# Order of matmuls in a narrow half, fewer fill matmuls between two stages, and a second load of x in pieces

## Chip, cores and metric

One core of one Trainium2 chip runs the whole program. The time is that of the device, in microseconds, from the first to the last instruction of one execution with what lies around it; the figure of a kernel is the median of its runs.

## What is computed

One layer of a streaming encoder on x (1, 256, 2048), everything in float32:

```python
h = rmsnorm(x, norm_mix_pre)
z, xbc, dt, q, k, v, q_idx, k_idx, w_idx, gates = split(h @ w_in)      # 18576 columns
y_ssm  = ssd_mixer(z, xbc, dt, ...) @ w_ssm_out                        # Mamba-2 branch, 4096 -> 2048
y_attn = dsa_mixer(q, k, v, q_idx, k_idx, w_idx) @ w_attn_out          # top-k attention, 2048 -> 2048
merged = sigmoid(gA) * y_ssm + sigmoid(gB) * y_attn
x = x + rmsnorm(merged @ w_mix_out, norm_mix_post)
h = rmsnorm(x, norm_ffn_pre)
x = x + rmsnorm((gelu(g) * val) @ w_down, norm_ffn_post)               # g, val = conv(h @ w_up)
```

Nearly all the work is products of 256 rows with about 340 MB of weights, each read once.

## The kernel before, in words

**Precision by two parts.** Each float32 weight w is split into a high part w_hi, rounded by ScalarE to the format that TensorE multiplies at one column per cycle (line 516), and a low part w_lo = w - w_hi, made by VectorE (line 892). Activations are split in the same way: a row tile of h_s, y_s or o_s holds 256 columns of high parts and 256 of low parts. A product is high times high, plus weight high times activation low, plus weight low times activation high.

**Halves.** The unit of the schedule is a *half*: 512 columns by 128 partitions of w_hi and of w_lo, 256 KB of weights. There are 1,224, and the table HALF (lines 74 to 81) numbers them by stage: Q 136, S 320, G 128, O 192, M 64, U 256, D 128. Four slots of w_hi and w_lo and four slots of raw weights (two halves each) go round. SP starts the loads of pair u when VectorE has finished half 2u - 7 (`slot_free`, line 309: lo_done at 2u - 6). ScalarE and VectorE work LEAD = 3 halves ahead of TensorE. ScalarE may overwrite a slot when TensorE has signalled `half_used` for the half four back.

**Narrow and wide.** In the stages Q, S and U the result is wanted with its channels on the partitions. There the weights are the stationary operand and the activations are streamed: `half`, lines 1448 to 1459, with two output tiles (banks b0 and b1) and two k-tiles. The high weights stream 512 columns (both parts of the activation), the low ones 256, into the bank's right half: eight matmuls, 4 x 512 + 4 x 256 = 3,072 columns. In the stages G, O, M and D the activations are stationary and 512 weight columns are streamed: `wide_half`, lines 1461 to 1472, six matmuls of 512 columns, three on one bank and then three on the other.

**Around the change.** Stage O ends with 16 halves on o_s; its halves on y_s are used 16 halves before stage M begins. The bytes of y_s are then used again: x_again (the second copy of x, for the residual sum), mix_gain and others lie on it. GpSimd loads them: it waits until TensorE has used all halves before M (line 475) and starts the two loads of x_again of 1 MB (line 477) and the 1 MB row of norm_mix_post, spread over the partitions (line 478). VectorE needs mix_gain behind half 16 of stage M (line 1308), and x_again at the end of stage M (line 1315), as does GpSimd (line 481). ffn_gain follows at the end of stage M (line 480).

Between M and U the new x (x2 = gained * scale + x_again) is made in pieces: VectorE takes seven (line 1320), GpSimd three (line 491). TensorE transposes it (h2_bank, line 1703, 16 tiles), ScalarE makes the high parts (line 795), VectorE the low parts (line 1329), and the first turn of U begins when the parts of tiles 0 and 1 are there, with the later tiles made between its halves. Ahead of the transposes TensorE runs six matmuls on `ones` and x_again into bank 7, whose result nobody reads (lines 1706 and 1707).

Of the kernel before, what the change touches and what calls it, by code (L numbers as in the profile page):

```python
# [73 lines left out]
HALF, TILE = {}, {}  # L74
# [46 lines left out]
def build(nc, x, norm_mix_pre, norm_mix_post, norm_ffn_pre, norm_ffn_post, w_in, b_gate, conv_xbc_w,  # L121
# [3 lines left out]
    with ctx:  # L125
        def sem(name):
            return ctx.enter_context(nc.semaphore(name))
# [7 lines left out]
        def place(name, shape, dt, at):  # L135
            size = 2 if dt == BF16 else 4
            for s in shape[1:]:
                size *= s
            at = (at + 31) // 32 * 32
            assert at + size <= ARENA, name  # L140
            return nc.alloc_sbuf_tensor_at(name, shape, dt, offset=base + at), at + size
# [37 lines left out]
        x_again, at = place("x_again", [P, 2, D], F32, RY)  # L179
# [61 lines left out]
        hi_done, lo_done, half_used = sem("hi_done"), sem("lo_done"), sem("half_used")  # L241
# [4 lines left out]
        par_in, small_in, skip_in, cs_kept, x_again_in = (sem(n) for n in (  # L246
            "par_in", "small_in", "skip_in", "cs_kept", "x_again_in"))
# [42 lines left out]
        x_view = x.rearrange("a (s p) d -> p (a s) d", p=P)  # L290
# [98 lines left out]
        def _(pool):  # L389
# [16 lines left out]
            for s in range(2):  # L406
                pool.tensor_scalar(x_rows[:, s, 3 * X_CHUNK:D], x_rows[:, s, 3 * X_CHUNK:D], stat[:, 0, 10 + s:11 + s], None,
                                   ALU.mult).then_inc(xn_pool, 1)
            rows = {"mix_pre": norm_mix_pre, "ffn_pre": norm_ffn_pre, "xbc_b": conv_xbc_b,
                    "ssm_norm": ssm_norm, "ffn_b": conv_ffn_b, "xbc_w": conv_xbc_w, "ffn_w": conv_ffn_w}  # L410
# [4 lines left out]
            for name, a in rows.items():  # L415
                src = rows_of(a)
                r0, n = PAR[name], src.shape[0]
# [54 lines left out]
                    pool.tensor_tensor(sq_sum[:], sq[:, 0, :] if n == 0 else sq_sum[:], sq[:, (n + 1) % 2, :],  # L472
                                       ALU.add).then_inc(sq_added, 1)

            pool.wait_ge(half_used, HALF["M"])
            for s in range(2):
                pool.dma_start(x_again[:, s, :], x_view[:, s, :]).then_inc(x_again_in, 16)
            pool.dma_start(mix_gain[:], norm_mix_post.rearrange("a d -> (a d)").partition_broadcast(P)).then_inc(gain_in[0], 16)
            pool.wait_ge(half_used, HALF["U"])
            pool.dma_start(ffn_gain[:], norm_ffn_post.rearrange("a d -> (a d)").partition_broadcast(P)).then_inc(gain_in[1], 16)  # L480
            pool.wait_ge(x_again_in, 32)
            pool.wait_ge(tile_out, TILE["M"] + 8)
            pool.wait_ge(inverted, 1)
            for n, (q, t) in enumerate(((1, 1), (3, 0), (3, 1))):
# [400 lines left out]
        def _(dve):  # L885
# [134 lines left out]
            with dve.Fori(0, 4) as i:  # L1020
                links.enter(i, 0, 8)
                for j in range(16):
# [10 lines left out]
                    if j % 8 == 7:  # L1033
                        for t in range(2):
                            k = j // 8
# [103 lines left out]
            with dve.Fori(0, GROUPS) as i:  # L1139
                links.enter(i, 0, 14)  # L1140
                for j in range(40):
# [41 lines left out]
                    if j % 8 == 7:  # L1183
                        k = j // 8
# [23 lines left out]
            with dve.Fori(0, GROUPS // 2) as i:  # L1208
                links.enter(i, 0, 2)
                for k in range(2):  # L1210
                    for j in range(16):
# [5 lines left out]
                        if 9 <= j < 13:  # L1217
                            n = 4 * k + j - 9
# [3 lines left out]
                        if 10 <= j < 14:  # L1222
                            n = 4 * k + j - 10
# [70 lines left out]
            def inverse(use):  # L1294

                dve.wait_ge(rooted, use + 1)
                dve.reciprocal(stat[:, use, 12:14], stat[:, use, 10:12]).then_inc(inverted, 1)
                dve.wait_ge(inverted, use + 1)
# [13 lines left out]
            with dve.Fori(1, 2) as i:  # L1312
                mix_turn(i, False)
            inverse(0)
            dve.wait_ge(x_again_in, 32)
            dve.wait_ge(tile_out, N + 8)

            def second_x(t, c0, c1):
# [120 lines left out]
            for n in range(8):  # L1439
                t, q = n // 4, n % 4  # L1440
# [6 lines left out]
        def _(pe):  # L1447
            def half(i, per, c, src, k0, b0, b1, start):

                pe.wait_ge(lo_done, i * per + (c + 1))  # L1450
                for k in range(2):
                    for t, b in enumerate((b0, b1)):
                        pe.matmul(bank[b][:], w_hi[:, c % 4, k, P * t:P * t + P], src[:, k0 + k, :],  # L1453
                                  start=start and k == 0, stop=False, skip_group_check=True)
                for k in range(2):
                    for t, b in enumerate((b0, b1)):
                        last = pe.matmul(bank[b][:, T:2 * T], w_lo[:, c % 4, k, P * t:P * t + P], src[:, k0 + k, 0:T],  # L1457
                                         start=False, stop=True, skip_group_check=True)
                last.then_inc(half_used, 1)
# [14 lines left out]
            def mm(o, a, b, start=True):  # L1474
                return pe.matmul(o, a, b, start=start, stop=True, skip_group_check=True)  # L1475
# [26 lines left out]
            for p in range(9):  # L1502
                if p >= 2:
                    pe.wait_ge(tile_out, 2 * p - 2)
                for j in range(8):
                    if p == 0:
                        pe.wait_ge(h_split, 2 * j + 2)
                    b = 2 * ((p + 1) % 2)
                    half(0, 0, 8 * p + j, h_s, 2 * j, b, b + 1, j == 0)
                    if p == 0 and j < 6:  # L1510
                        for kt in (2 * j + 4, 2 * j + 5):
# [38 lines left out]
            with pe.Fori(0, 4) as i:  # L1550
                for k in range(2):
                    pe.wait_ge(tile_out, i * 4 + (18 + 2 * k - 2))
                    for j in range(8):
                        half(i, 16, 72 + 8 * k + j, h_s, 2 * j, 2 * k, 2 * k + 1, j == 0)
# [148 lines left out]
                    last = pe.transpose(bank[4 + kt % 4][:, P * t:P * t + P], x2[:, t, P * kt:P * kt + P], ident[:])  # L1703
                last.then_inc(h2_mm, 1)

            for n in range(6):
                mm(bank[7][:], ones[:], x_again[:, 0, 0:WIDE])
            for kt in range(4):
                h2_bank(kt)
# [55 lines left out]
```

## Time and profile before

| | |
|---|---|
| median of 3 runs | 1825.42 us (1824.72 to 1825.81) |
| the profiled execution | 1825.45 us, of which the span of the trace is 1823.8 us |
| busy: TensorE | 1797.7 us, 99% |
| busy: VectorE | 1305.3 us, 72% |
| busy: ScalarE | 1098.7 us, 60% |
| busy: GpSimd | 159.3 us, 9% |
| HBM read | 342 MB, 189 GB/s over the span |

In the rows PE is TensorE, PEld its weight loads, DVE VectorE, ACT ScalarE, POOL GpSimd and SP SyncE. Matmuls are pipelined: the length of one is its time in flight, and the distance from start to start is what it costs. The timeline merges neighbours of one kind into one line with a count. The idle time in brackets counts from the end of the flight before. The clock is the one granted to TensorE, as a share of 2.4 GHz.

### The profile page before, as it was taken

Reading aid. Unit: us, or ns where it says so; the run is one execution under the profiler, and the core shown is the slowest. Engines: PE = TensorE matmul, PEld = TensorE weight load, DVE = VectorE, ACT = ScalarE, POOL = GpSimd, SP = SyncE. Lnnn points to the kernel's source line nnn. Section 1 sums busy time; section 2 is a strip of 40 time slices with the busy share of each in tenths; the row PEclk is TensorE's granted clock in tenths of the full one; section 3 lists DMA queues with packets and bytes.
Section 4 is the critical chain, followed back from the end, with each engine's and each line's share of the span. In section 5 each row is a group of like instructions: output and inputs, shape, how many; then the busy total and the mean of one; then the engine's idle time right before and its main releaser. Section 6 shows DMA issues by size and latency. Waiting matters only on the chain.

```text
span 1823.8 us, 34379 instructions
## 1 busy us (share of the span) xinstructions
PE 1797.7 (99%) x9519; PEld 1528.3 (84%) x9519; DVE 1305.3 (72%) x2436; ACT 1098.7 (60%) x2147; POOL 159.3 (9%) x230
## 2 busy tenths in 40 slices
PE   8999999999999999999999999999999999999997
PEld 7888888888888888888888888877888888888886
DVE  6766687888888788777755555555787888875555
ACT  6554566666666666666755455544766666665443
POOL 2000001110110010111100000001111111110000
PEclk9999999999999999999999999999999999999999
DMA  7656666766666665666666666676566666666664
GB/s 215 205 165 186 184 180 179 202 184 177 196 184 190 178 202 163 189 201 202 198 198 191 186 195 189 213 230 187 159 188 189 189 186 188 189 184 190 195 193 148
DMA packets 362387, 345.00 MB, mean 189 GB/s; under 512 B 29072, under 2 KB 291360, under 8 KB 361568
## 3 DMA queue, kind: packets, MB, share of 16 engines
q1 hardware_dynamic: 357024, 325.14, 60.1%
q0 software_dynamic: 5280, 19.23, 3.3%
q8 instruction: 25, 0.41, 0.1%
q14 instruction: 26, 0.21, 0.0%
q10 hardware_dynamic: 32, 0.01, 0.0%
HBM read 342.13 MB, written 2.16 MB: 189 GB/s over the span
## 4 chain that ended last, share of the span: by engine, by line
PE 90%; DVE 4%; issue 2%; ACT 2%; DMA 1%; DVEq 0%; ACTq 0%; SPq 0%
PE bank L1468 37%; PE bank L1453 32%; PE bank L1457 16%; PE bank L1475 3%; ACT w_hi L516 1%; DVE w_lo L892 1%; DVE cc L1080 1%; DMA raw<-in_w_mix_out 1%; PE bank L1592 0%; DVE xc L1091 0%; DMA x_rows<-in_x 0%; DVE upad L898 0%; DVE out_t L1442 0%; DVE bc L1091 0%; ACT cc L626 0%
## 5 line engine op out<-in xcount | busy, mean ns | idle before, releaser
L892 DVE TENSOR_TENSOR w_lo<-raw,w_hi 128x512 fp32r<-128x512 f32 x1224 | 855.0, 707 | 471.1 <-ACT w_hi L516 464.4
L516 ACT ACTIVATE w_hi<-raw 128x512 fp32r<-128x512 f32 x1224 | 760.7, 629 | 505.5 <-PE bank L1468 273.3
L1453 PE MATMUL bank<-h_s,w_hi 128*128 128x512 f32 x1824 | 508.2, 400 | 0.8 <-DVE h_s L910 0.8
L1453 PEld LDWEIGHTS bank<-h_s,w_hi 128*128 128x128 f32 x1824 | 312.3, 189 | 48.7 <-issue 5.2
L1468 PE MATMUL bank<-w_hi,y_s 128*128 128x512 f32 x1024 | 316.7, 389 | 0.0
L1457 PEld LDWEIGHTS bank<-h_s,w_lo 128*128 128x128 f32 x1824 | 278.9, 188 | 39.0
L1457 PE MATMUL bank<-h_s,w_lo 128*128 128x256 f32 x1824 | 289.3, 280 | 0.0
L1453 PE MATMUL bank<-o_s,w_hi 128*128 128x512 f32 x1024 | 280.3, 395 | 2.4 <-issue 0.9
L1468 PE MATMUL bank<-w_hi,h_s 128*128 128x512 f32 x768 | 240.8, 392 | 2.3 <-DVE w_lo L892 2.3
L1468 PEld LDWEIGHTS bank<-w_hi,y_s 128*128 128x128 f32 x1024 | 192.2, 188 | 39.7
L1468 PE MATMUL bank<-w_lo,y_s 128*128 128x512 f32 x512 | 199.2, 389 | 0.0
L1453 PEld LDWEIGHTS bank<-o_s,w_hi 128*128 128x128 f32 x1024 | 174.9, 189 | 26.7 <-DVE o_s L1329 1.2
L1457 PEld LDWEIGHTS bank<-o_s,w_lo 128*128 128x128 f32 x1024 | 157.1, 189 | 21.9
L1468 PEld LDWEIGHTS bank<-w_hi,h_s 128*128 128x128 f32 x768 | 144.1, 188 | 33.1 <-issue 2.4
L1457 PE MATMUL bank<-o_s,w_lo 128*128 128x256 f32 x1024 | 162.9, 281 | 0.0
L1468 PE MATMUL bank<-w_lo,h_s 128*128 128x512 f32 x384 | 149.4, 389 | 0.0
L1468 PEld LDWEIGHTS bank<-w_lo,y_s 128*128 128x128 f32 x512 | 96.1, 188 | 20.0
L523 ACT ACTIVATE tmp<-bank 128x256 f32<-128x256 f32 x178 | 58.6, 381 | 79.2 <-PE bank L1457 79.2
L1468 PEld LDWEIGHTS bank<-w_lo,h_s 128*128 128x128 f32 x384 | 72.1, 188 | 14.9
L500 POOL TENSOR_TENSOR fpad<-fpad,rstd 128x256 f32<-128x256 f32 x64 | 53.0, 850 | 310.4 <-DVE fpad L898 285.8
L1468 PE MATMUL bank<-w_hi,o_s 128*128 128x512 f32 x256 | 79.4, 389 | 0.0
L1080 DVE SCALAR_TENSOR_TENSOR cc<-upad,par,cc 128x256 f32<-128x256 f32 x144 | 59.0, 478 | 0.0
(217 smaller groups left out, 1238.5 us busy)
## 6 DMA issues: line engine op xcount, KB each, us to landing
raw<-in_w_in SPq DMA_DIRECT2D x576, 256.0 KB, 3.0
raw<-in_w_up SPq DMA_DIRECT2D x256, 256.0 KB, 3.2
raw<-in_w_ssm_out SPq DMA_DIRECT2D x128, 256.0 KB, 3.3
raw<-in_w_down SPq DMA_DIRECT2D x128, 256.0 KB, 3.4
raw<-in_w_attn_out SPq DMA_DIRECT2D x64, 256.0 KB, 3.3
raw<-in_w_mix_out SPq DMA_DIRECT2D x64, 256.0 KB, 3.4
cs_rows<-cs_dram POOLq DMA_DIRECT2D x16, 512.0 KB, 5.1
cs_rows<-cs_dram POOLq DMA_DIRECT2D x16, 256.0 KB, 6.1
```

The source lines that it names most:

```text
L500: pool.tensor_tensor(u, u, rstd[:], ALU.mult).then_inc(u_scaled, 1)
L516: act.activation(w_hi[:, c % 4, :, :], raw[:, slot, 2 * m:2 * m + 2, :], ACT.Copy).then_inc(hi_done, 1)
L523: act.activation(tmp[:, n % 2, :], bank[b][:, 0:T], ACT.Copy).then_inc(main_out, 1)
L892: dve.tensor_tensor(w_lo[:, c % 4, :, :], raw[:, (c // 2) % 4, 2 * (c % 2):2 * (c % 2) + 2, :], w_hi[:, c % 4, :, :].bitcast(F32), ALU.sub ...
L1080: ins = dve.scalar_tensor_tensor(out=cc[:, t, :], in0=upad[:, t, n:n + T], scalar=col("xbc_w", tile[t] + n * 48), in1=cc[:, t, :], op0=ALU ...
L1453: pe.matmul(bank[b][:], w_hi[:, c % 4, k, P * t:P * t + P], src[:, k0 + k, :], start=start and k == 0, stop=False, skip_group_check=True)
L1457: last = pe.matmul(bank[b][:, T:2 * T], w_lo[:, c % 4, k, P * t:P * t + P], src[:, k0 + k, 0:T], start=False, stop=True, skip_group_check= ...
L1468: last = pe.matmul(bank[b + t][:], src[:, kt, at + P * t:at + P * t + P], w, start=kt == 0 and w is hi and at == 0, stop=True, skip_group_ ...
L1475: return pe.matmul(o, a, b, start=start, stop=True, skip_group_check=True)
```

## The change

Three edits. In `half` the loop over the two banks becomes the outer one: high k0, high k1, low k0, low k1 on b0, and then the same on b1. In front of the transposes of stage U the unread matmuls are three in place of six. GpSimd loads x_again in four pieces of 64 partitions by 8 KB, behind halves M - 16, M - 10, M - 4 and M + 2, and mix_gain behind half M + 6; the waits on x_again_in go from 32 to 64.

```diff
@@ gpsimd
-            pool.wait_ge(half_used, HALF["M"])
-            for s in range(2):
-                pool.dma_start(x_again[:, s, :], x_view[:, s, :]).then_inc(x_again_in, 16)
+            for n in range(4):
+                s, rows = n // 2, slice(64 * (n % 2), 64 * (n % 2) + 64)
+                pool.wait_ge(half_used, HALF["M"] - 16 + 6 * n)
+                pool.dma_start(x_again[rows, s, :], x_view[rows, s, :]).then_inc(x_again_in, 16)
+            pool.wait_ge(half_used, HALF["M"] + 6)
             pool.dma_start(mix_gain[:], norm_mix_post.rearrange("a d -> (a d)").partition_broadcast(P)).then_inc(gain_in[0], 16)
             pool.wait_ge(half_used, HALF["U"])
             pool.dma_start(ffn_gain[:], norm_ffn_post.rearrange("a d -> (a d)").partition_broadcast(P)).then_inc(gain_in[1], 16)
-            pool.wait_ge(x_again_in, 32)
+            pool.wait_ge(x_again_in, 64)
@@ vector
-            dve.wait_ge(x_again_in, 32)
+            dve.wait_ge(x_again_in, 64)
@@ tensor, half
-                for k in range(2):
-                    for t, b in enumerate((b0, b1)):
+                for t, b in enumerate((b0, b1)):
+                    for k in range(2):
                         pe.matmul(bank[b][:], w_hi[:, c % 4, k, P * t:P * t + P], src[:, k0 + k, :],
                                   start=start and k == 0, stop=False, skip_group_check=True)
-                for k in range(2):
-                    for t, b in enumerate((b0, b1)):
+                    for k in range(2):
                         last = pe.matmul(bank[b][:, T:2 * T], w_lo[:, c % 4, k, P * t:P * t + P], src[:, k0 + k, 0:T],
                                          start=False, stop=True, skip_group_check=True)
@@ tensor, before stage U
-            for n in range(6):
+            for n in range(3):
                 mm(bank[7][:], ones[:], x_again[:, 0, 0:WIDE])
```

## Rows read from the trace of the kernel before

**Rows 1.** The page's busy time of TensorE (us, share of the span, instructions).

```profile
PE 1797.7 (99%) x9519; PEld 1528.3 (84%) x9519; DVE 1305.3 (72%) x2436; ACT 1098.7 (60%) x2147; POOL 159.3 (9%) x230
```

**Rows 2.** The page's costliest groups: names, shapes, count, busy us, mean ns, idle before.

```profile
L1453 PE MATMUL bank<-h_s,w_hi 128*128 128x512 f32 x1824 | 508.2, 400 | 0.8 <-DVE h_s L910 0.8
...
L1468 PE MATMUL bank<-w_hi,y_s 128*128 128x512 f32 x1024 | 316.7, 389 | 0.0
```

**Rows 3.** Timeline of TensorE in stage U; columns: start us, length us, engine, line, what.

```profile
1289.26 1.09 PE L1453 MATMUL bank<-o_s,w_hi 128*128 128x512 f32 x4
...
1294.86 0.39 PE L1453 MATMUL bank<-o_s,w_hi 128*128 128x512 f32 x1
```

**Rows 4.** Timeline of TensorE in stage M, behind the pause; idle before in brackets.

```profile
1193.37 0.47 PE L1468 MATMUL bank<-w_hi,h_s 128*128 128x512 f32 x1 [2.04 <-DVE w_lo L892]
1193.68 0.40 PE L1468 MATMUL bank<-w_lo,h_s 128*128 128x512 f32 x1
...
1194.38 0.39 PE L1468 MATMUL bank<-w_lo,h_s 128*128 128x512 f32 x1
...
1196.44 0.39 PE L1468 MATMUL bank<-w_lo,h_s 128*128 128x512 f32 x1
...
1197.12 0.39 PE L1468 MATMUL bank<-w_lo,h_s 128*128 128x512 f32 x1
```

**Rows 5.** The chain of waits in order of time: start us, length us, what.

```profile
1180.83 11.02 DMA raw<-in_w_mix_out
...
1276.89 1.35 DVE x L1320
```

**Rows 6.** Timeline of all engines at the handover from M to U.

```profile
1266.94 5.32 PE L1475 MATMUL bank<-x_again,ones 128*128 128x512 f32 x12
...
1268.86 2.68 DVE L1320 SCALAR_TENSOR_TENSOR x<-gained,stat,x_again 128x256 f32<-128x256 f32 x4
...
1272.10 1.04 PE L1703 MATMUL bank<-ident,x 128*128 128x128 f32 x8
...
1273.02 0.88 DVE L1329 SCALAR_TENSOR_TENSOR o_s<-bank,par,o_s 128x256 fp32r<-128x256 f32 x2 [1.46 <-ACT o_s L795]
...
1274.00 1.16 PE L1453 MATMUL bank<-o_s,w_hi 128*128 128x512 f32 x4 [0.87 <-issue]
...
1278.69 1.20 PE L1453 MATMUL bank<-o_s,w_hi 128*128 128x512 f32 x4 [0.77 <-DVE o_s L1329]
```

**Rows 7.** Timeline of GpSimd at the start of stage M and at the start of U.

```profile
1177.13 1.08 POOL L477 DMA_DIRECT2D x_again<-in_x  x2 [280.29 <-PE bank L1468]
...
1276.39 1.29 POOL L491 TENSOR_TENSOR x<-gained,x_again 128x512 f32<-128x512 f32 x1
```

**Rows 8.** DMA issues between 1170 and 1210 us: KB each, median us to landing.

```profile
x_again<-in_x POOLq DMA_DIRECT2D x2, 1024.0 KB, 9.3
mix_gain<-in_norm_mix_post POOLq DMA_DIRECT2D x1, 1024.0 KB, 13.5
```

**Rows 9.** Windows before and behind the load: busy us of each engine, clock, DMA share, GB/s.

```profile
1178.00:1192.00 14.00, 13.33 (x63) 10.78 (x61) 7.38 (x14) 4.96 (x12) 0.72 (x2) 1.00 0.94 344
1155.00:1177.00 22.00, 22.00 (x99) 18.22 (x98) 12.30 (x19) 10.96 (x17) 0.00 (x0) 1.00 0.64 191
```

**Rows 10.** DMA issues between 1260 and 1290 us: the other gain row.

```profile
ffn_gain<-in_norm_ffn_post POOLq DMA_DIRECT2D x1, 1024.0 KB, 5.9
```

**Rows 11.** Timeline of TensorE in stage S, two halves behind other work.

```profile
247.52 1.08 PE L1453 MATMUL bank<-h_s,w_hi 128*128 128x512 f32 x4
...
248.91 1.09 PE L1453 MATMUL bank<-h_s,w_hi 128*128 128x512 f32 x4
```

**Rows 12.** Timeline of TensorE at the start and the end of the program.

```profile
8.38 2.93 PE L1475 MATMUL bank<-ident,ones 128*128 128x128 f32 x12 [3.97 <-DMA x_rows<-in_x]
...
1812.58 0.39 PE L1468 MATMUL bank<-w_hi,y_s 128*128 128x512 f32 x1
```

**Rows 13.** One window behind the last matmul: busy us of each engine, clock, DMA.

```profile
1817.00:1818.00 1.00, 0.00 (x0) 0.00 (x0) 1.00 (x3) 0.00 (x0) 0.00 (x0) 0.82 1.04 381
```

## The prediction

> **What bounds the kernel now.** I began with the share of the span that each engine is busy. TensorE is busy 99% of it [rows 1], so time can only be won where TensorE pauses, or where its matmuls follow each other more slowly than they might. Next I looked at the costliest groups of instructions, to see which matmuls there are. The narrow halves (line 1453 high, line 1457 low) and the wide halves (line 1468) both stream 3,072 columns per half, but a 512-column matmul is in flight for 400 ns in the narrow ones and 389 ns in the wide ones [rows 2]. In flight is not the distance between two matmuls; that is read from the timeline of TensorE. Four narrow halves lie between 1289.26 and 1294.86 us, so 1.40 us each [rows 3]. Three wide matmuls take 0.68 us (1196.44 to 1197.12) [rows 4], so a wide half of six takes 1.36 us. The narrow half needs two more matmuls for the same columns. If each matmul costs its columns at 2.4 GHz plus the wide one's surplus (226.7 - 213.3 = 13.3 ns), a narrow half should need 3,072 / 2.4 + 8 x 13.3 = 1,387 ns. So some 13 ns per half (1,400 against 1,387) are unexplained. There are 712 narrow halves (136 + 320 + 256): 9 to 10 us in all.
>
> Last, the pauses of TensorE. One is at 1193.37 us, 2.04 us long, until the low part of a weight is ready [rows 4]. The chain of waits leads it back to one load of the mix weights that took 11.02 us to land [rows 5]. The other is the handover from stage M to stage U at 1267 to 1279 us [rows 6].
>
> **The second load of x.** GpSimd issues both 1 MB loads at 1177.13 [rows 7], and the 1 MB gain row right behind them. They land in 9.3 us (median) and 13.5 us [rows 8]. From 1178 to 1192 the DMA engines are 0.94 busy at 344 GB/s; in the 22 us before they were 0.64 busy at 191 GB/s [rows 9]. So the burst fills the engines, the weight load inside it is late, and TensorE stops. The change starts the four 0.5 MB pieces after halves M-16, M-10, M-4 and M+2, 6 x 1.36 = 8.2 us apart, and the gain row after M+6. Three of the four pieces now fall into stage O. Each adds 0.5 MB in 8.2 us, or 64 GB/s on top of 191: 255, well under 344. The tightest place is the last piece and the gain row, 1.5 MB from M+2 on; the spare rate 344 - 191 = 153 GB/s takes them in some 10 us. They are due at M+16, 14 x 1.36 = 19 us later. The row of the other gain, issued alone in the same form, landed in 5.9 us [rows 10]. A load is started six halves (8.2 us) before ScalarE needs it (line 309), and ScalarE leads TensorE by three halves; the 11.02 us one ate both. So I take the stall as gone. Its worth: 2.04 us idle, plus what restarting costs. The first matmul after it is 0.31 us before the second (1193.37 to 1193.68) where 0.227 is usual, and the next triples take 0.70 and then 0.687 us (2.06 / 3) instead of 0.68 [rows 4]. Together 2.04 + 0.16 (the pipeline's own 0.39 in flight less 0.227) + 0.08 + 0.04 = 2.3 us. Bounds: 0 (stall stays, because the gain row alone is enough) and 2.3. I take **-2.3**. Behind GpSimd's new waits there are only its own DMA issues, 0.54 us each [rows 7]; its next arithmetic comes after stage M. SP's queue is not moved.
>
> **Three warm matmuls in place of six.** Each mm on fp32 operands gives two records, 12 in all, and TensorE goes from 1266.94 to the first transpose at 1272.10, so one record costs 5.16 / 12 = 0.43 us [rows 6]. Six fewer end at 1266.94 + 6 x 0.43 = 1269.52. VectorE's first two pieces of x2 are done at 1268.86 + 2 x 0.67 = 1270.20, and all four at 1271.54. So transposes 0 and 1 run at 1270.2 and 2 and 3 at 1271.6, in place of 1272.10 to 1273.14. What is late next is VectorE: ScalarE now rounds 0 and 1 in time, and the low parts come right behind VectorE's own four pieces, 1271.6 + 2 x 0.44 = 1272.5 instead of 1273.90. The first matmul of U starts at about 1272.6, not 1274.00: 1.4 us earlier. Further on, the chain of VectorE and ScalarE (second pieces of x2 between low parts, which run longer while GpSimd works on its own, until 1276.39 + 1.29 = 1277.7) sets the start of the third half, now 1278.69 [rows 6]. My chain for it: first half 1272.6 to 1274.05, transposes 4 and 5 to 1274.5, ScalarE to 1275.1, low part of 4 to 1275.55, a piece of x2 at 1.35 us [rows 5] to 1277.0, low part of 5 to 1277.45. I take **-1.2**; bounds 0 (GpSimd's pieces, not moved, end the wait) and -2.6 (all removed records on the path). On the removed work's other role see the clock, below.
>
> **The order of the narrow half.** Nothing is added or removed: the same eight matmuls, the same wait ahead and the same signal behind the last one. Before, they are four high ones on alternating banks, then four low ones on alternating banks; now high, high, low, low on one bank, then on the other. The old order leaves a bank 8 times per half, the new one twice. No row shows the new order, so the price is bounded by near rows:
> - Best case, 1,387 ns: the floor worked out above. It is seen: the half from 247.52 to 248.91 takes 1.39 us [rows 11]. That is 13 to 16 ns less than usual, x 712 = -9 to -11 us.
> - Worst case. What costs the surplus may be the change of cadence and not the bank. After the stall the wide halves, three matmuls on one bank each, also run at 0.70 us per triple before they settle at 0.68 [rows 4]: 6.7 ns too much per matmul, with no alternation. In the narrow half each run of four low matmuls breaks the cadence, and the high ones behind it pay. The new order breaks it twice per half. If every high matmul pays 7 to 8 ns and the low ones give nothing back, a half takes 1,387 + 4 x 8 = 1,419 ns, +13 to +15 ns after what low matmuls now give back: +10 us.
> Between them I take **0**: by the nearest rows two dear high matmuls per run make 4 x 6.7 = 27 ns of surplus [rows 4], of which pairs of low matmuls, started late, win back some 3 to 7 ns each, twice. That is 13 to 20 ns of surplus, against 13 to 16 today. Uncertainty of this case by itself: +-2 us.
>
> **The sum.** The profiled execution took 1825.45 us (span 1823.8), the median of the runs is 1825.42, so they stand together. 1825.4 - 2.3 - 1.2 + 0 = **1821.9 us**, -0.19%. About 0.2% (3.65 us) is what a measurement of this kernel can tell from no change, so this case lies on that border, at 1819.5 to 1824.5.
>
> **Rivals.**
> 1. *The banks were the cost* (chance 0.30). For it: the 11 ns of longer flight in exactly the family that alternates [rows 2]. Against: the slow triples on one bank [rows 4]. It gives 1821.9 - 10 = 1812 us.
> 2. *The broken cadence costs mildly more* (0.17): half of the worst case, +5 us, 1827. With the gains it ends within 0.2%.
> 3. *The broken cadence costs fully* (0.09). One mechanism, in `half`: each return from low to high columns makes the next two high matmuls dear, and there are two returns per half instead of one. Price +10 to +15 ns x 712 = +7 to +11 us: 1829 to 1833, slower than before. It decides from (3.65 + 3.5) / 712 = 10 ns per half on.
> 4. *The clock falls in the handover* (0.05). The fills are there to keep TensorE at work. Now it would have only eight transposes between 1269.5 and 1272.6. After the last matmul (1812.58) the granted clock averaged 0.82 in 1817 to 1818 [rows 12, 13], so it fell inside that stretch, over four microseconds into a full rest, longer than this one. At the start of the program twelve 128-column matmuls took 2.93 us, 0.24 each, where the eight transposes at 1272.10 took 0.13 each [rows 6, 12]: the lower level, 1.2 GHz, doubles the price. If it fell for the first two narrow halves it would cost up to 2.8 us, and the handover would lose what it gained: 1823.5 to 1825. The Trainium skill ("TensorE: Matmul & The Clock Gate", Part 4: PE-mode transpose) says that transposes do not count as work for the clock gate, which makes the rest longer than it looks; by that rule the time would be the one just given. No row of this kernel shows it.
> 5. *The loads do not do what is meant* (0.04): the gain row alone, or a piece in stage O, makes a weight load late again. 1824 to 1826.
> The forecast itself has 0.35.
>
> **How the numbers follow.** Faster by over 0.2% (below 1821.8): rival 1, half of the forecast case, and the good tail of small savings in the order: 0.30 + 0.18 + 0.04 = 0.52. Slower by over 0.2% (above 1829.1): rival 3, 0.09. The rest, 0.39, is within 0.2%. The range must take in rival 1 and the mild rival 2: from 1811 to 1828.5. It leaves out most of rival 3 and little else.
>
> **What would show it.** Stage M: no pause of TensorE near 1192 us, weight loads landing in under 8 us, the DMA share nowhere above 0.9. Handover: six records of line 1707, and the first matmul of U some 5.7 us after the last of M instead of 7.1. Order: four narrow halves in 5.60 us if I am right; 5.55 with a mean flight near 389 ns at line 1453 if the banks were the cost; over 5.64 for rival 3. A granted clock below 1.00 behind the handover would mean rival 4. I am wrong if narrow halves change by more than 3 ns each, or if the pause in stage M only moves.

## The result

| | before | changed kernel |
|---|---|---|
| median | 1825.81 us (5 runs, 1824.72 to 1827.15) | 1817.67 us (5 runs, 1817.3 to 1817.81) |
| ratio of the runs | | 0.9956, 95% interval 0.9946 to 0.9967 |
| profiled execution | 1825.45 us, span 1823.8 | 1817.3 us, span 1815.6 |

8.1 us are gained, 0.44%, where 3.5 were forecast. The time lies inside the range (1811 to 1828.5), on the side that had the larger chance, but 4.2 us below the central value of 1821.9. The range is 17.5 us wide so as to take in rivals 1 and 2, and its lower end was set by rival 1, whose mechanism the experiments refute. So the hit is in part luck. The runs also lie closer together: 0.5 us from first to last in place of 2.4.

**The page after.** TensorE's line of the page, and two of the costliest groups; compare [rows 1] and [rows 2]. Lines have moved: the high matmuls stand on line 1455 now, the low ones on 1458 and the wide ones on 1469. The kernels of the experiments have other line numbers again.

```profile
PE 1790.9 (99%) x9513; PEld 1521.5 (84%) x9513; DVE 1305.2 (72%) x2436; ACT 1100.1 (61%) x2147; POOL 164.7 (9%) x232
...
L1455 PE MATMUL bank<-h_s,w_hi 128*128 128x512 f32 x1824 | 584.3, 402 | 1.1 <-DVE h_s L912 1.0
...
L1458 PE MATMUL bank<-h_s,w_lo 128*128 128x256 f32 x1824 | 359.4, 278 | 0.0
```

Busy time fell by 6.8 us, the span by 8.2. The 512-column matmul of the narrow halves is in flight for 402 ns on average, more than the 400 before, and yet the halves are shorter, as the starts below show. So the flight of 400 against 389 ns in the wide halves, on which the prediction's first rival rested, was no measure of what a matmul costs.

**Where the time came from.** The view of one line gives the first and the last start of its instructions. For the high matmuls of the narrow halves after the change:

```profile
L1455 PE MATMUL bank<-h_s,w_hi x1824: 389/396/583, 13.3 to 731.7; 128*128 128x512 f32 x183
...
L1455 PE MATMUL bank<-o_s,w_hi x1024: 387/396/504, 1268.1 to 1630.1; 128*128 128x512 f32 x171
```

The same view of the kernel before has 13.4 to 733.5 us and 1274.0 to 1638.0 us. The last matmul starts at 1812.58 before [rows 12] and at 1804.5 after. With the first of the warm matmuls, 1266.94 before [rows 6] and 1262.55 after, that makes four parts:

| part | before | after | gain |
|---|---|---|---|
| Q and S, first to last high matmul | 720.1 | 718.4 | 1.7 |
| G, O and M, from there to the first warm matmul | 533.4 | 530.9 | 2.6 |
| handover, first warm matmul to first matmul of U | 7.1 | 5.5 | 1.6 |
| U, first to last high matmul | 364.0 | 362.0 | 2.0 |

The sum is 7.9 us; D takes the same time within 0.2 us. Two of the four parts are the narrow halves, and there the forecast was nothing.

**The narrow half.** The timeline of TensorE in stage U, to set beside [rows 3]:

```profile
1283.44 0.62 PE L1455 MATMUL bank<-o_s,w_hi 128*128 128x512 f32 x2
1283.90 0.40 PE L1458 MATMUL bank<-o_s,w_lo 128*128 128x256 f32 x2
1284.14 0.63 PE L1455 MATMUL bank<-o_s,w_hi 128*128 128x512 f32 x2
...
1291.80 0.40 PE L1455 MATMUL bank<-o_s,w_hi 128*128 128x512 f32 x1
```

Two high matmuls in flight, two low ones, and again. From 1283.44 to 1291.80 there are six halves: 8.36 / 6 = 1.393 us each, where it was 1.40. Two highs take 0.46 to 0.47 us, two lows 0.23 to 0.24. A few lines are a small sample, so the starts were averaged over the longest stretch of stage U that no other work interrupts, 228 halves: 1.403 us per half before, 1.393 after.

**The load.** The timeline of GpSimd (two of its five issues), the time to landing (KB, median us), and the one wait of ScalarE for a mix weight (us in total, times, longest). They are to be set beside [rows 7] and [rows 8]:

```profile
1153.30 0.54 POOL L478 DMA_DIRECT2D x_again<-in_x  x1 [258.52 <-PE bank L1469]
...
1184.12 0.55 POOL L480 DMA_DIRECT2D mix_gain<-in_norm_mix_post  x1 [5.83 <-PE bank L1469]
```

```profile
x_again<-in_x POOLq DMA_DIRECT2D x4, 512.0 KB, 6.3
mix_gain<-in_norm_mix_post POOLq DMA_DIRECT2D x1, 1024.0 KB, 7.9
```

```profile
ACT w_hi L518 <- DMA raw<-in_w_mix_out: 1.7, 1, 1.7
```

The pieces land in 6.3 us and the gain row in 7.9, in place of 9.3 and 13.5. ScalarE still waits once for a mix weight, 1.7 us, but it is three halves ahead and TensorE does not feel it: the pause of 2.04 us [rows 4] is gone. The longest load of a mix weight behind 1178 us takes 7.8 us, where it was 11.0. The DMA engines are full for a while all the same, behind the last piece and the gain row (busy us of each engine, then clock, DMA share, GB/s):

```profile
1190.00:1192.00 2.00, 2.00 (x10) 1.67 (x9) 0.66 (x1) 0.36 (x1) 0.00 (x0) 1.00 1.01 373
```

**The handover.** The timeline of all engines, to set beside [rows 6]:

```profile
1262.55 2.74 PE L1476 MATMUL bank<-x_again,ones 128*128 128x512 f32 x6
...
1264.47 2.68 DVE L1322 SCALAR_TENSOR_TENSOR x<-gained,stat,x_again 128x256 f32<-128x256 f32 x4
...
1265.41 0.66 PE L1704 MATMUL bank<-ident,x 128*128 128x128 f32 x4
...
1267.21 0.66 PE L1704 MATMUL bank<-ident,x 128*128 128x128 f32 x4 [1.14 <-DVE x L1322]
...
1268.06 0.70 PE L1455 MATMUL bank<-o_s,w_hi 128*128 128x512 f32 x2 [0.19 <-issue]
...
1272.05 0.73 PE L1455 MATMUL bank<-o_s,w_hi 128*128 128x512 f32 x2
...
1274.88 0.73 PE L1455 MATMUL bank<-o_s,w_hi 128*128 128x512 f32 x2 [0.67 <-DVE o_s L1331]
```

Six records of warm matmuls, then transposes at 1265.41, and now TensorE waits for x2 between the second and the third tile (0.66 us in flight from 1265.41, the next at 1267.21). The first matmul of U comes 5.51 us after the first warm one (7.06 before), the third half 9.50 us (11.75 before).

### The profile page after: what moved, and what is told of

The parts are those of the page before. It is cut to its first block, busy times and chain, and to the rows that moved or that the text cites. A ratio compares the mean times of both kernels' runs of the same rounds, so it can differ in the third digit from the quotient of the medians.

```text
span 1815.6 us, 34369 instructions
## 1 busy us (share of the span) xinstructions
PE 1790.9 (99%) x9513; PEld 1521.5 (84%) x9513; DVE 1305.2 (72%) x2436; ACT 1100.1 (61%) x2147; POOL 164.7 (9%) x232
## 4 chain that ended last, share of the span: by engine, by line
PE 91%; DVE 4%; issue 2%; ACT 2%; DMA 0%; DVEq 0%; ACTq 0%; SPq 0%
PE bank L1469 38%; PE bank L1455 33%; PE bank L1458 16%; PE bank L1476 3%; ACT w_hi L518 1%; DVE cc L1082 1%; DVE w_lo L894 1%; PE bank L1593 0%; DVE xc L1093 0%; DMA x_rows<-in_x 0%; DVE upad L900 0%; DVE x L1322 0%; DVE out_t L1444 0%; ACT cc L628 0%; PE bank L1660 0%
## 5 line engine op out<-in xcount | busy, mean ns | idle before, releaser
L1455 PE MATMUL bank<-h_s,w_hi 128*128 128x512 f32 x1824 | 584.3, 402 | 1.1 <-DVE h_s L912 1.0
L1458 PEld LDWEIGHTS bank<-h_s,w_lo 128*128 128x128 f32 x1824 | 342.6, 188 | 81.2
L1458 PE MATMUL bank<-h_s,w_lo 128*128 128x256 f32 x1824 | 359.4, 278 | 0.0
L1455 PE MATMUL bank<-o_s,w_hi 128*128 128x512 f32 x1024 | 322.6, 396 | 1.7 <-DVE w_lo L894 0.8
L1455 PEld LDWEIGHTS bank<-h_s,w_hi 128*128 128x128 f32 x1824 | 278.9, 189 | 8.0 <-issue 4.3
L1458 PEld LDWEIGHTS bank<-o_s,w_lo 128*128 128x128 f32 x1024 | 192.4, 188 | 45.5
L1458 PE MATMUL bank<-o_s,w_lo 128*128 128x256 f32 x1024 | 201.3, 278 | 0.0
L1455 PEld LDWEIGHTS bank<-o_s,w_hi 128*128 128x128 f32 x1024 | 155.9, 189 | 2.7 <-DVE o_s L1331 1.2
```

## The experiments

All times are medians; each run is set against runs of the kernel before on the same chip, 1825.55 to 1826.09 us.

### One edit at a time: e1, e2, e3

The edits are those of the change, each alone: e1 the new order, e2 the count of warm matmuls, e3 the pieces of x with the later gain row. The first lines of each:

```diff
-                for k in range(2):
-                    for t, b in enumerate((b0, b1)):
+                for t, b in enumerate((b0, b1)):
+                    for k in range(2):
```

```diff
-            for n in range(6):
+            for n in range(3):
```

```diff
-            pool.wait_ge(half_used, HALF["M"])
-            for s in range(2):
+            for n in range(4):
...
+                pool.wait_ge(half_used, HALF["M"] - 16 + 6 * n)
```

> Only the order of the narrow half is changed (six warm matmuls and the loads of x as before). In the trace of the whole change, stretches of narrow halves that nothing interrupts run at 1.394 us per half, against 1.400 to 1.403 before, and the narrow stages are about 4.1 us shorter. If the order alone makes that, this kernel is 4 us faster than before (1821.5 to 1822), its clean narrow halves take 1.394 us, and the pause of 2.0 us in stage M and the six warm matmuls are unchanged. If part of the 4 us came from the other two edits, it is less than 2 us.

> Only the warm matmuls are cut from six to three. My prediction: first matmul of U 1.4 us earlier, 1.2 us kept at the third half, total -1.2 us. Rival: the new x2 pieces of GpSimd or the clock take it back, total 0, with the wait for x2 or a clock under 1.00 in the handover.

> Only the second load of x is split and spread. My prediction: the pause of 2.04 us in stage M goes, total -2.3 us. Rival: the gain row right behind the last piece is enough to keep half of it: -1 us or less, and TensorE waits for a low part at about 1192 us.

| | median us | ratio, 95% interval | from 1825.61 | runs |
|---|---|---|---|---|
| e1_order | 1822.69 | 0.9978 (0.9969 to 0.9987) | -2.9 | 11, 1821.01 to 1824.24 |
| e2_fills | 1824.71 | 0.9994 (0.9985 to 1.0003) | -0.9 | 11, 1823.43 to 1827.93 |
| e3_load | 1823.10 | 0.9986 (0.9977 to 0.9996) | -2.5 | 11, 1823.07 to 1823.52 |

Only e3 has runs that agree, and its median gives 2.5 us for the load against 2.3 forecast. Its trace has no pause in stage M. e2's interval takes in no change at all; its trace shows the handover as in the change (the first matmul of U 5.50 us after the first warm one). e1's clean halves have the new 1.393 us, but its median misses the 1821.5 to 1822 that were expected. e1 and e2 keep the burst, and their runs spread over 3 and 4.5 us. The reason stands in e1's waits of TensorE (us in total, times, longest) and in two windows of stage M (busy us of each engine, then clock, DMA share, GB/s):

```profile
PE bank L1468 <- DVE w_lo L892: 3.6, 2, 3.3
```

```profile
1188.00:1192.00 4.00, 1.52 (x7) 0.94 (x5) 0.03 (x1) 0.69 (x2) 0.00 (x0) 1.00 0.93 353
...
1194.00:1196.00 2.00, 2.00 (x6) 1.61 (x5) 0.47 (x1) 0.46 (x1) 0.00 (x0) 0.50 0.66 154
```

In this execution the pause was 3.3 us long, where the execution before the change shows 2.04, and behind it the granted clock was 0.50, the 1.2 GHz level. The length of the pause does not decide that alone. e4, the next kernel, keeps the burst too; its profile has a pause of 2.01 us, no longer than that of the kernel before, and the clock is down behind it:

```profile
1191.72 0.48 PE L1468 MATMUL bank<-w_hi,h_s 128*128 128x512 f32 x1 [2.01 <-DVE w_lo L892]
```

```profile
1192.00:1194.00 2.00, 2.00 (x6) 1.60 (x5) 1.38 (x3) 0.55 (x2) 0.00 (x0) 0.51 0.43 113
```

So the burst does not cost a fixed amount. It opens a pause whose length differs between executions (1.7 us in e2's profile), and in some executions, not in others with a pause as long, the clock falls on top.

The mean granted clock that is on record for every execution sorts the spread. Medians in us, number of executions in brackets:

| | mean clock 0.998 | mean clock below 0.998 |
|---|---|---|
| before | 1825.28 (19) | 1827.30 (14) |
| e1_order | 1821.30 (5) | 1823.44 (6) |
| e2_fills | 1823.70 (6) | 1826.07 (5) |
| e3_load | 1823.10 (11) | none |
| e4_altbank | 1821.28 (6) | 1823.22 (5) |

In the first column the order alone is worth 4.0 us, the warm matmuls 1.6 and the load 2.2. In the kernels with the burst the second column is about 2 us longer, and with the spread load (e3) it is empty. So spreading wins twice: the pause, and the 2 us that 14 of 33 executions of the kernel before lost besides. From e5 on the versions have the spread loads (but for e10).

### Banks or cadence: e4, e5

e4 has the cadence of the change (two high, two low, twice) but goes to the other bank with every matmul. All else is as before the change. In the new loop header `low` says high or low, `k` is the k-tile and `t` the bank.

```diff
-                for k in range(2):
-                    for t, b in enumerate((b0, b1)):
...
+                for low, k, t in [(0, 0, 0), (0, 0, 1), (1, 0, 0), (1, 0, 1),
+                                  (0, 1, 0), (0, 1, 1), (1, 1, 0), (1, 1, 1)]:
```

> The cadence of the change without its banks: high, high, low, low twice per half, but every matmul on the other bank than the one before it (k-tile by k-tile), nothing else changed. If the cadence (how many high matmuls follow each other) sets the time, clean narrow halves take 1.394 us as in e1_order and the kernel is 4 us faster than before. If leaving a bank costs the time, they take 1.400 to 1.403 us and the kernel is as before.

1821.88 us (0.9977, 0.9968 to 0.9986), as e1 within their spread; in the executions with the mean clock 0.998 the two are 0.02 us apart. The timeline of TensorE in stage U:

```profile
1288.53 0.63 PE L1457 MATMUL bank<-o_s,w_hi 128*128 128x512 f32 x2
1288.99 0.40 PE L1454 MATMUL bank<-o_s,w_lo 128*128 128x256 f32 x2
1289.23 0.63 PE L1457 MATMUL bank<-o_s,w_hi 128*128 128x512 f32 x2
...
1292.71 0.62 PE L1457 MATMUL bank<-o_s,w_hi 128*128 128x512 f32 x2
```

From 1288.53 to 1292.71 there are three halves of 1.393 us, with eight changes of bank in each. Averaged over all halves of a stretch but its first, e4 and e1 are equal: 1.395 us in the stages Q and S, 1.394 in U. The banks cost nothing that can be measured here.

e5 is the opposite: the whole change, but with four highs and then four lows, which stay on a bank for two matmuls.

```diff
+                for low, k, t in [(0, 0, 0), (0, 1, 0), (0, 0, 1), (0, 1, 1),
+                                  (1, 0, 0), (1, 1, 0), (1, 0, 1), (1, 1, 1)]:
```

> The whole change but for the cadence: four high matmuls and then four low ones as before, in the bank order of the change as far as that goes (k-tiles 0 and 1 on one bank, then on the other, first high, then low). If the cadence sets the time, clean narrow halves go back to 1.400 to 1.403 us and the kernel takes 1821.7 us. If fewer changes of bank were worth something by themselves, they lie between 1.387 and 1.398 us and the kernel is at 1817 to 1820.

1821.73 us (nine runs, 1821.37 to 1821.86; ratio 0.9974, 0.9964 to 0.9984). The timeline of TensorE in U:

```profile
1285.13 1.08 PE L1459 MATMUL bank<-o_s,w_hi 128*128 128x512 f32 x4
1286.06 0.64 PE L1456 MATMUL bank<-o_s,w_lo 128*128 128x256 f32 x4
...
1292.14 1.09 PE L1459 MATMUL bank<-o_s,w_hi 128*128 128x512 f32 x4
```

Five halves in 7.01 us, 1.402 each. Four changes of bank in place of eight, and the old time. Against the change itself (1817.67) the cadence alone is worth 4.06 us, on runs that agree within half a microsecond; e1 and e4 gave 4.0. e5 is also e3 with three warm matmuls in place of six (and another order of banks, which costs nothing by e4). So the warm matmuls are worth 1823.10 - 1821.73 = 1.4 us where no burst disturbs.

### Which cadence: e6, e7

Both are the whole change with other runs of high and low.

e6 runs high, low, high, low on b0 and then on b1; e7 runs four high and four low in even halves, four low and four high in odd ones, which makes runs of eight across two halves.

```diff
+                for low, k, t in [(0, 0, 0), (1, 0, 0), (0, 1, 0), (1, 1, 0),
+                                  (0, 0, 1), (1, 0, 1), (0, 1, 1), (1, 1, 1)]:
```

```diff
+                for low, k, t in ([(0, 0, 0), (0, 0, 1), (0, 1, 0), (0, 1, 1), (1, 0, 0), (1, 0, 1), (1, 1, 0), (1, 1, 1)] if c % 2 == 0 else
+                                  [(1, 0, 0), (1, 0, 1), (1, 1, 0), (1, 1, 1), (0, 0, 0), (0, 0, 1), (0, 1, 0), (0, 1, 1)]):
```

> The whole change, with the narrow half as high, low, high, low on one bank and then on the other. In the change the two high matmuls of a pair cost 233 ns each and the two low ones 114 to 116. Theory (each high matmul behind another high one is late, the low one behind it wins that back): with a low one behind every high one nothing is left over, a half takes 1.387 to 1.390 us and the kernel 1814 to 1815.5 us. Rival (each change between high and low costs by itself, four changes per half turn into eight): 1.400 us or more, 1822 us or more.

> The whole change, with runs of eight in place of two: even halves run four high and four low matmuls, odd halves four low and four high. Theory (the cost grows with the high matmuls that follow each other): a half takes 1.400 to 1.407 us, the kernel 1822 to 1826 us. Rival (each change between high and low costs, and there is one per half in place of four; long runs settle at the wide half's spacing): 1.387 to 1.390 us, 1814 to 1815.5 us.

e6: 1827.84 us (1.0009, 0.9999 to 1.0019). e7: 1818.82 us (0.9958, 0.9941 to 0.9974). The timelines of TensorE in stage U, first e6, then e7:

```profile
1295.00 0.40 PE L1459 MATMUL bank<-o_s,w_hi 128*128 128x512 f32 x1
1295.23 0.28 PE L1456 MATMUL bank<-o_s,w_lo 128*128 128x256 f32 x1
1295.35 0.40 PE L1459 MATMUL bank<-o_s,w_hi 128*128 128x512 f32 x1
...
1300.30 0.60 PE L1477 MATMUL bank<-diag,ones 128*128 128x128 f32 x4
...
1301.08 0.40 PE L1459 MATMUL bank<-o_s,w_hi 128*128 128x512 f32 x1
...
1303.51 0.39 PE L1459 MATMUL bank<-o_s,w_hi 128*128 128x512 f32 x1
```

```profile
1286.18 2.00 PE L1460 MATMUL bank<-o_s,w_hi 128*128 128x512 f32 x8
1288.02 1.12 PE L1457 MATMUL bank<-o_s,w_lo 128*128 128x256 f32 x8
...
1291.77 1.55 PE L1460 MATMUL bank<-o_s,w_hi 128*128 128x512 f32 x6
```

In e6 fifteen pairs lie between 1295.00 and 1300.30: 0.353 us each, 1.413 us per half. Behind the four small matmuls at 1300.30 the same code runs seven pairs in 2.43 us (1301.08 to 1303.51), 0.347 each or 1.389 us per half. So the spacing is not a property of an instruction alone: after an interruption the same sequence can fall into another, shorter rhythm. In stage U it is rare, 10 of some 240 halves. e7 has four halves in 5.59 us (1286.18 to 1291.77), 1.397.

In e7 the lows in a row settle at 120.0 ns from start to start (the third to the eighth) and the highs at 226.7 (the sixth to the eighth), the two spacings from which the prediction's floor of 1.387 us was worked out. That lets each cadence be taken apart. The averages are those of the long stretch of stage U, 228 halves in each kernel:

| highs in a row | us per half | four highs over 4 x 226.7, ns | four lows under 4 x 120.0, ns | kernel, us |
|---|---|---|---|---|
| 1 (e6) | 1.413 | 40 | 13 | 1827.84 |
| 2 (the change) | 1.393 | 26 | 19 | 1817.67 |
| 4 (e5, and the kernel before) | 1.403 | 23 | 6 | 1821.73 |
| 8 (e7) | 1.397 | 14 | 4 | 1818.82 |

From four in a row to two, the highs become 3 ns dearer per half and the lows 13 ns cheaper. The whole gain of the order lies in the low matmuls.

Both of my theories failed here. "The low one behind each high one wins it back" called for the shortest half in e6, which is the longest. "The cost grows with the highs in a row" called for 1822 or more in e7. "Each change between high and low costs" explains e6 and e7, but then two in a row would have to be worse than four. The best is neither end. The table says where the time goes, but I have no rule that gives it.

### What the warm matmuls are for: e8, e9, e11, e12

e8 leaves all warm matmuls out.

```diff
-            for n in range(3):
-                mm(bank[7][:], ones[:], x_again[:, 0, 0:WIDE])
```

> The whole change with no warm matmuls at all (the unread matmuls on ones are left out). If x2 sets the start of the transposes, the three that are left cost nothing, and this kernel takes 1817.7 us as the change does, as long as the clock stays at 1.00. If the warm matmuls keep the clock up, it falls within the handover and the kernel takes 1819 us or more, with a mean clock under 0.998 and transposes of twice the spacing.

1818.64 us (four runs, 1818.58 to 1818.73; ratio 0.9957, 0.994 to 0.9974), 1.0 us more than with three. Windows of e8 around the handover, and its timeline of TensorE:

```profile
1264.00:1266.00 2.00, 0.41 (x2) 0.42 (x3) 1.92 (x6) 0.95 (x2) 0.44 (x1) 0.92 1.03 304
...
1268.00:1270.00 2.00, 2.00 (x8) 1.69 (x7) 1.57 (x4) 0.90 (x2) 1.92 (x2) 0.50 0.08 29
1270.00:1272.00 2.00, 2.00 (x9) 1.83 (x8) 0.00 (x0) 0.41 (x1) 1.92 (x3) 0.50 0.00 0
```

```profile
1265.59 1.06 PE L1705 MATMUL bank<-ident,x 128*128 128x128 f32 x4 [2.70 <-DVE x L1322]
...
1268.23 1.19 PE L1459 MATMUL bank<-o_s,w_hi 128*128 128x512 f32 x2
...
1269.65 1.05 PE L1459 MATMUL bank<-o_s,w_hi 128*128 128x512 f32 x2
```

The transposes start no earlier than in the change (three us behind the last matmul of M, as x2 wants it), but the clock is down. At 0.50 a pair of highs and a pair of lows take 1.42 us (1268.23 to 1269.65), twice the usual.

e9 was the changed kernel once more, e11 the same with the gain row first and the pieces of x later:

```diff
+            for n in range(2):
+                at = slice(D // 2 * n, D // 2 * n + D // 2)
+                pool.wait_ge(half_used, HALF["M"] - 16 + 6 * n)
+                pool.dma_start(mix_gain[:, at], norm_mix_post[:, at].rearrange("a d -> (a d)").partition_broadcast(P)).then_inc(gain_in[0], 16)
...
+                pool.wait_ge(half_used, HALF["M"] + 8 + 12 * n)
...
+            pe.wait_ge(x_again_in, 64)
```

> The changed kernel itself, once more, beside the next two on the same chip: 1817.7 us, a spread under 1 us.

> The whole change, but the gain row goes first, in two halves of 0.5 MB at M - 16 and M - 10, and the four pieces of x follow inside stage M, at M + 8, M + 20, M + 32 and M + 44, where nothing else is loaded. No two extra loads are in flight together. The 0.3 us that TensorE still waits in stage M of the changed kernel should go with its restart cost: 1817.0 to 1817.4 us. If that wait is not from the loads, 1817.7 us.

1817.71 us (1817.37 to 1818.67; ratio 0.9954, 0.9941 to 0.9968) and 1817.66 (1817.62 to 1818.66; 0.9955, 0.9941 to 0.9968). e11 brings nothing. The 0.3 us of waiting that it was to remove is not in stage M at all: TensorE waits it at 736.7 us, at the start of stage G, and at 738.8 us in the kernel before. My expectation had put it in the wrong place. What both bring is one run of five that is 1 us longer, and in both it is the profiled one. Windows of e9 in the handover:

```profile
1268.00:1270.00 2.00, 1.81 (x8) 1.38 (x7) 1.75 (x4) 0.84 (x2) 1.92 (x2) 0.71 0.29 119
1270.00:1272.00 2.00, 2.00 (x9) 1.83 (x8) 0.08 (x1) 0.59 (x2) 1.92 (x3) 0.50 0.01 4
```

The clock was 0.50 here, with three warm matmuls. In the profile of the changed kernel, with the same instructions, it stayed at 1.00. Eight kernels were profiled with three warm matmuls ahead of the transposes; in two profiles (e9, e11) the clock fell in the handover, in six (the change, e2, e5, e6, e7, e10) it stayed at 1.00. So with three, some executions lose the clock and pay 1 us.

e12 adds one unread matmul in the place where TensorE waits for x2 anyway.

```diff
             for kt in range(4):
+                if kt == 2:
+                    mm(bank[7][:], ones[:], x_again[:, 0, 0:WIDE])
                 h2_bank(kt)
```

> The whole change, with one more unread matmul of the same kind between the transposes of tiles 1 and 2, where TensorE waits 1.1 us for x2 anyway. In two profiled executions with three warm matmuls ahead (e9 and e11) the granted clock was 0.50 for a few microseconds in the handover, and the first turn of U took about 1 us longer than in the profile of the change. Theory: the extra matmul (two records of 0.43 us) fits into the wait, costs nothing, and fills the gap; the clock stays at 1.00 in the profile, the median is 1817.3 to 1817.7 us and no run is over 1818.2 us. Rival: TensorE is too little at work between 1265.4 and 1268 us all the same, and some runs still take 1818.7 us; or the extra matmul delays tiles 2 and 3 and every run is 0.2 us or more longer.

1817.63 us, five runs from 1817.54 to 1817.82; ratio 0.9955, 0.9941 to 0.9969. The timeline of TensorE, and windows of the handover:

```profile
1265.70 0.66 PE L1704 MATMUL bank<-ident,x 128*128 128x128 f32 x4
1266.19 1.02 PE L1476 MATMUL bank<-x_again,ones 128*128 128x512 f32 x2
1267.51 0.66 PE L1704 MATMUL bank<-ident,x 128*128 128x128 f32 x4 [0.29 <-DVE x L1322]
```

```profile
1262.00:1266.00 4.00, 3.88 (x14) 1.93 (x13) 3.44 (x9) 2.74 (x7) 0.86 (x2) 1.00 0.81 187
1266.00:1270.00 4.00, 3.52 (x20) 2.31 (x19) 3.69 (x8) 1.68 (x4) 3.92 (x3) 1.00 0.56 223
1270.00:1274.00 4.00, 3.92 (x25) 3.29 (x24) 3.25 (x5) 2.72 (x6) 3.09 (x3) 1.00 0.00 0
```

The two records fit between the transposes, 0.29 us of waiting are left, and the clock stays at 1.00. As a median it is the changed kernel, and none of its five runs was long. Five are too few to show that none will be. Of the fifteen runs of the change, e9 and e11 two were long, so five in a row without one come about half the time by chance; and both long ones were on one chip, e12 on another.

### The burst elsewhere: e10

The whole change, but x and the gain row go out together at half M - 16.

```diff
+            pool.wait_ge(half_used, HALF["M"] - 16)
+            for s in range(2):
+                pool.dma_start(x_again[:, s, :], x_view[:, s, :]).then_inc(x_again_in, 16)
```

> The whole change, but the second load of x and the gain row go out together, 3 MB at once, at half M - 16. The place is as early as in the change, the spreading is gone. Theory (the burst fills the DMA engines and one weight load lands too late): TensorE pauses in stage O some 10 to 15 us behind the issue, the kernel takes 1819.5 to 1820.5 us, and its runs spread by 1 us or more again. Rival (it was only the start of stage M, where VectorE and ScalarE also make the merged tiles): no pause, 1817.7 us or less.

1821.76 us (eleven runs, 1820.14 to 1823.46; 0.9977, 0.9968 to 0.9986), more than the 1819.5 to 1820.5 expected. The waits of TensorE, and the link of its chain of waits:

```profile
PE bank L1468 <- DVE w_lo L892: 2.8, 2, 2.5
```

```profile
1155.75 11.89 DMA raw<-in_w_attn_out
```

The same pause, 2.5 us, now in stage O and behind a load of attention weights that took 11.89 us. The place does not matter, the 3 MB at once do. With the change's 1817.7 beside it, spreading is worth 4.1 us in the median here: the pause and the clock, whose mean is below 0.998 in nine of the eleven runs (in the profile it is 0.50 from 1170 to 1172 us).

## Why the prediction was right, and where it was not

**The load.** The step from 3 MB at once to "one load late" to "TensorE stops" is shown by e3 (pause gone) and by e10 (pause back in another stage). The size was right for executions that keep the clock: 2.2 us (1825.28 to 1823.10), forecast 2.3; the medians give 2.5. Two things were missing. The pause is not constant: I took its 2.04 us from one profiled execution, and others had 1.7 and 3.3. And I charged nothing for the clock, which the burst cost in 14 of 33 executions of the kernel before. One sign was wrong as well: the DMA share was to stay below 0.9 and reached 1.0 at 373 GB/s in the change (1190 to 1192 us). Full DMA engines are thus not enough for a pause; what went away with the 3 MB is a weight load of 11 us. The longest one is now 7.8 us, just under the 8 that were forecast.

**The warm matmuls.** The prediction's "5.7 us behind the last of M instead of 7.1" counts from the first warm matmul (1272.6 - 1266.94, and 7.06). Counted so, it is 5.51 us: 1.55 us earlier, where 1.4 were forecast. The third half was to gain 1.2 us; it gained 11.75 - 9.50 = 2.2, and the fourth only 13.79 - 12.33 = 1.5 (from 1280.73 - 1266.94 before and 1274.88 - 1262.55 after), and that is what was kept. e3 against e5 gives 1.4. The term was mis-sized by 0.2 to 0.3 us. Rival 4, the clock, had 0.05. It came true in some executions (e9, e11), and with no warm matmuls at all in e8, whose four runs agree. Its rows on the lower level were poorly chosen, since the trace's windows show no lower clock where the twelve first matmuls run; e8 shows the doubling, 1.42 for 0.70 us. The rival was priced at up to 2.8 us, and cost 1.0. The trace of e9 shows why. Its third half of U starts 1.8 us later behind the first than in the change (5.81 against 3.99), its fourth only 1.0 us later (7.86 against 6.82), for there the change waits 0.67 us for VectorE and e9 does not. The Trainium skill says that transposes do not count as work for the clock gate ("TensorE: Matmul & The Clock Gate", Part 4: PE-mode transpose). That agrees with e9 and e12, but six profiles with the same transposes kept the clock, and no run here separates the rule from plain idleness.

**The order of the narrow half** is the step that failed. "Between them I take 0" should have been -4.1 us (1821.73 of e5 against 1817.67), near the middle between 0 and the best case of -10. By the prediction's own last sign ("wrong if narrow halves change by more than 3 ns each") it was wrong here: they changed by 10. It was also a gain that no rival named. Rival 1 had the banks, which cost nothing (e4, e5); rivals 2 and 3 had the cadence, but as a loss. Two things in it were right: it is the cadence and not the bank, and the rows of the wide halves behind a pause [rows 4] were the evidence for that. What was wrong is one side of the bookkeeping. I charged 27 ns per half for the dear highs, and the change has 26. I let the pairs of lows win back 3 to 7 ns, twice, and they win back 19 in all. That leaves 7 ns over the floor where 13 to 20 were forecast, against 17 with four in a row.

Over 712 halves 10 ns would be 7 us; only 4.1 came. In the stages Q and S other work interrupts the 456 halves 106 times. The first half behind an interruption was 1.500 us before and is 1.506 now, the second 1.394 both times (the 1.39 us of [rows 11] is one of them); only from the third on is there a gain, 1.404 to 1.395. Hence 1.7 us for 456 halves there, and 2.0 for the 256 of U.

**The sum.** Forecast 0 - 2.3 - 1.2 = -3.5. Measured, each step between two kernels that differ in that edit: -2.5 (before against e3), -1.4 (e3 against e5), -4.1 (e5 against the change), together -8.0 of the 8.1. Half of the gain is the term that was put at 0. The time lay in the range because the range was wide, and below 1821.8 for another reason than the 0.30 of rival 1.

**Left open:** why highs cost 227 ns in a settled wide half and 228 to 237 in a mixed one, and why two in a row are best. That the same code has two rhythms (e6) says that what ran before has a part in it; how, no run here shows. Open too is what decides whether the clock falls behind a pause, since pauses of equal length did both.

## What to carry to other kernels

Spare bandwidth in the mean (the DMA engines were 0.64 busy ahead of the burst) says nothing about a burst: set the time to landing of every large side load against the lead of the stream beside it, and spread it where it reaches the lead. Judge matmuls by the distance of their starts, not by their time in flight, and try the order of long and short ones as a measured choice. Where TensorE must wait, a filler in the gap itself cost nothing here (e12), while six in front of it cost 1.4 us more than three; whether the one in the gap keeps the clock safely is not settled. The worth of a filler is seen in the granted clock of several executions, not of one. And where runs spread, sort them by their mean clock before taking a median.

## What the runs showed of the hardware

- Runs of 512- and 256-column matmuls with equal work per half take 1.393, 1.397, 1.403 or 1.413 us by how they alternate, whatever the banks (e4, e5, e6, e7, the change); the same sequence of e6 took 1.413 and, behind a short interruption, 1.389. In long runs the starts settle at 226.7 ns for 512 columns and 120.0 for 256 (e7).
- Pauses of 3.3 us (e1), 2.5 (e10) and 2.01 (e4) in an otherwise full stream of matmuls were followed by a granted clock of 0.50; pauses of 2.04 (before) and 1.74 (e2) were not. With small matmuls in the pause of the handover the clock fell in two of eight profiles; with one longer matmul among them it did not in the one profile taken (e12).
- A side load of 3 MB at once raised a single 256 KB load to between 10.7 and 12.3 us in five profiles, where the median is 3.4; four loads of 0.5 MB, 8 us apart, and then one of 1 MB left the longest at 7.8 us, and TensorE did not pause, though the DMA share reached 1.0.
